# Key products and values of a recurrence kept with its two heads exchanged, on the off-diagonal 64x64 tiles of TensorE

## The reference, cut to what matters

```
def step(state, inp):
    r_t, w_t, k_t, v_t, a_t, b_t = inp
    sa = einsum("bhij,bhj->bhi", state, a_t)
    state = state * w_t + sa[..., None] * b_t + v_t[..., None] * k_t
    return state, einsum("bhij,bhj->bhi", state, r_t)
```

## Time and profile before

| | |
|---|---|
| median of 3 runs | 3216.4 us (3216.02 to 3230.35) |
| the profiled execution, its own time | 3214.21 us |
| its span, first to last instruction | 3212.4 us |
| TensorE matmul busy | 2920.5 us, 91% |
| VectorE busy | 1461.4 us, 45% |
| ScalarE busy | 438.4 us, 14% |
| mean granted TensorE clock | 0.956 |

### The profile page before, as it was taken

One profiled execution on the slowest core, in us unless ns is written; L12 is line 12 of the kernel. 1 busy time (PEld: TensorE's weight loads), 2 busy tenths in 40 slices (PEclk: granted clock), 3 DMA queues, 4 the chain that ended last, 5 costly groups with the idle time before them and its releaser, 6 DMA issues.

```text
span 3212.4 us, 50284 instructions
## 1 busy us (share of the span) xinstructions
PE 2920.5 (91%) x22141; PEld 2107.7 (66%) x22141; DVE 1461.4 (45%) x2546; ACT 438.4 (14%) x860; POOL 261.9 (8%) x372
## 2 busy tenths in 40 slices
PE   4997999999999888889979979999999998886998
PEld 4775877777775544367757758777777745443775
DVE  3542265566655756213025323656664567552001
ACT  0000132121211112000000001312111122120000
POOL 6000011001100101010000010101010010000000
PEclk7998999999999989989989989999998999998999
DMA  8782332112225432363548724322222263323342
GB/s 310 275 313 105 125 129 98 67 52 97 77 71 185 138 133 79 131 255 127 173 172 317 261 99 143 112 70 73 70 77 70 70 226 125 130 79 131 121 146 100
DMA packets 226043, 444.09 MB, mean 138 GB/s; under 512 B 7432, under 2 KB 102214, under 8 KB 225824
## 3 DMA queue, kind: packets, MB, share of 16 engines
q1 hardware_dynamic: 211136, 395.59, 34.8%
q0 software_dynamic: 12960, 38.98, 3.7%
q10 hardware_dynamic: 1728, 6.29, 0.5%
HBM read 422.88 MB, written 17.96 MB: 137 GB/s over the span
## 4 chain that ended last, share of the span: by engine, by line
PE 69%; DVE 14%; issue 10%; DMA 4%; ACT 2%; POOL 1%; SPq 0%; DVEq 0%; POOLq 0%; ACTq 0%
PE ps L966 67%; DVE scratch L1868 5%; DVE scratch L1871 2%; DVE scratch L1874 2%; DMA ring<-in_ffn_w 2%; DMA scratch<-fill_scratch 1%; DVE merged L2067 1%; DVE hT L1871 1%; ACT scratch L1566 1%; DVE scratch L2081 1%; DVE gbc L1874 1%; DMA scratch<-acs_scratch 1%; DMA ring<-in_w_in 0%; PE ps L998 0%; DVE x L1868 0%
## 5 line engine op out<-in xcount | busy, mean ns | idle before, releaser
L966 PE MATMUL ps<-hT,ring 128*128 128x256 f32 (+1 forms) x4992 | 1169.4, 389 | 32.5 <-DVE hT L1871 31.0
L966 PE MATMUL ps<-scratch 64*64 64x32 f32 (+6 forms) x14112 | 1023.9, 260 | 89.0 <-ACT scratch L1815 27.9
L966 PEld LDWEIGHTS ps<-hT,ring 128*128 128x128 f32 (+1 forms) x4992 | 941.0, 192 | 199.2 <-DVE hT L1871 33.1
L966 PEld LDWEIGHTS ps<-scratch 64*64 64x64 f32 (+2 forms) x14112 | 717.7, 145 | 433.3 <-issue 243.4
L1868 DVE TENSOR_TENSOR scratch<-scratch,ps 128x256 f32<-128x256 f32 (+3 forms) x304 | 153.5, 505 | 933.1 <-ACT scratch L1576 671.6
L966 PE MATMUL ps<-ring,hT 128*128 128x256 f32 (+1 forms) x1280 | 433.0, 485 | 6.6 <-DVE hT L2491 4.9
L966 PEld LDWEIGHTS ps<-ring,hT 128*128 128x128 f32 x1280 | 239.6, 195 | 157.3 <-issue 129.5
L1868 DVE TENSOR_TENSOR scratch<-scratch 128x512 f32<-128x512 f32 (+5 forms) x438 | 288.3, 658 | 73.2 <-DMA scratch<-acs_scratch 26.3
L966 PE MATMUL ps<-ring,scratch 128*128 128x512 f32 x512 | 239.4, 607 | 2.9 <-DVE scratch L1871 2.3
L1874 DVE SCALAR_TENSOR_TENSOR scratch<-scratch,ccol 128x1024 f32<-128x1024 f32 x126 | 164.2, 1303 | 4.5
L966 PEld LDWEIGHTS ps<-ring,scratch 128*128 128x128 f32 x512 | 95.5, 196 | 98.8 <-issue 93.3
(11 more groups left out here) (217 smaller groups left out, 1440.4 us busy)
## 6 DMA issues: line engine op xcount, KB each, us to landing
ring<-in_w_in SPq DMA_DIRECT2D x56, 2048.0 KB, 7.9
ring<-in_ffn_w SPq DMA_DIRECT2D x88, 1024.0 KB, 9.9
scratch<-in_ada_w SPq DMA_DIRECT2D x36, 2048.0 KB, 14.3
scratch<-in_ffn_w SPq DMA_DIRECT2D x44, 1024.0 KB, 4.9
scratch<-acs_scratch POOLq DMA_DIRECT2D x32, 512.0 KB, 4.9
ring<-in_w_branch_mamba SPq DMA_DIRECT2D x8, 2048.0 KB, 8.6
scratch<-fill_scratch SPq DMA_DIRECT2D x4, 2048.0 KB, 13.6
ring<-in_w_branch_rwkv SPq DMA_DIRECT2D x4, 2048.0 KB, 11.0
```

The lines of the kernel that those rows point to most:

```text
L966: return pe.matmul(o, lhsT, rhs, start=start, stop=stop)
```

## The change

A second helper, `by_other_head`, addresses the off-diagonal 64x64 tiles: with `to_other` the result of a head lands on the other head's partitions, and without it the operands of the other head's partitions give the result on a head's own. The keys' products (`kdec`) and the transposed values (`vtm`) are written to the other head's partitions, and `values_share` brings them back. So `mk`, `ktm` and `vtm` are kept with the heads exchanged. The `kdec` products are issued between the `bdec` and the `ar` product of each chunk; for d=1 all of these wait for `m2_evac` too. In the recurrent steps the value products are issued among the products on the diagonal tiles: the state's share moves from behind the u product to behind the s hand-over, the next r's share goes between the two u products, and all output shares of the values stand in j=0's first group. ScalarE's and VectorE's programs are the same.

```diff
+                def by_other_head(o, lhsT, rhs, start=True, stop=True, to_other=False):
+                    for h in range(2):
+                        hh, oh = slice(L * h, L * h + L), slice(L - L * h, 2 * L - L * h)
+                        at, of = (oh, hh) if to_other else (hh, oh)
+                        ins = mm(o[at], lhsT[of], rhs[of], start, stop)
+                    return ins
...
-                        by_head(ps[:, 0, c * L:(c + 1) * L], rkv[:, 16 + q, c * L:(c + 1) * L], stack_i[:, :])
+                        by_other_head(ps[:, 0, c * L:(c + 1) * L], rkv[:, 16 + q, c * L:(c + 1) * L], stack_i[:, :], to_other=True)
...
                             pe.wait_ge(*btm_evac(l, u))
+                            pe.wait_ge(*m2_evac(l, u))
                         for c in range(CH):
                             bank, at = 2 + c // 2, (c % 2) * 3 * L
-                            by_head(ps[:, bank, at:at + 3 * L], bdec[:, d, c, :], ar[:, d, c, :, :].rearrange("p u t -> p (u t)"))
+                            moving = ar[:, d, c, :, :].rearrange("p u t -> p (u t)")
+                            by_head(ps[:, bank, at:at + 3 * L], bdec[:, d, c, :], moving)
+                            keys = by_other_head(ps[:, 2 + bank, at:at + 3 * L], kdec[:, d, c, :], moving, to_other=True)
+                            if c == CH - 1:
+                                keys.then_inc(m2_done.sem, 1)
                             at = 6 * L + (c % 2) * L
                             ins = by_head(ps[:, bank, at:at + L], ar[:, d, c, 0, :], bdec[:, d, c, :])
                         ins.then_inc(m1_done.sem, 1)
-                        if d:
-                            pe.wait_ge(*m2_evac(l, u))
-                        for c in range(CH):
-                            bank, at = 4 + c // 2, (c % 2) * 3 * L
-                            ins = by_head(ps[:, bank, at:at + 3 * L], kdec[:, d, c, :], ar[:, d, c, :, :].rearrange("p u t -> p (u t)"))
-                        ins.then_inc(m2_done.sem, 1)
...
-                        return by_head(o, weights, vtm[:, c, :], start, stop)
+                        return by_other_head(o, weights, vtm[:, c, :], start, stop)
...
+                    def state_share(j, d):
+                        c = chunk(d, j)
+                        values_share(ps[:, 0, d * L:(d + 1) * L], ktm[:, d, c, :], c, d == 0, False)
...
                                 by_head(ps[:, 6, c * L:(c + 1) * L], ar[:, d, c, 1, :], st8[:, j, d, :], False, False)
+                                if j < CH - 1:
+                                    state_share(j, d)
                         else:
-                            for c in range(CH):
-                                values_share(ps[:, 6, c * L:(c + 1) * L], mk[:, 0, c, L:2 * L], c, c == 0, False)
+                            for d in range(2):
+                                for c in range(CH):
+                                    values_share(ps[:, 6, c * L:(c + 1) * L], mk[:, d, c, L:2 * L], c, d == 0 and c == 0, False)
+                            for d in range(2):
+                                state_share(j, d)
                         fill(p, f"r{j}")
                         pe.wait_ge(*r_evac(l, 4 * p + j + 1))
                         for d in range(2):
-                            ins = by_head(ps[:, 5, d * L:(d + 1) * L], dd[:, d, 1, chunk(d, j), :], rs[:, d, :])
-                        ins.then_inc(u_done.sem, 1)
-                        if j < CH - 1:
-                            for d in range(2):
+                            if d and j < CH - 1:
                                 c = chunk(d, j + 1)
                                 values_share(ps[:, 4, d * L:(d + 1) * L], mk[:, d, c, 0:L], c, d == 0, False)
-                            for d in range(2):
-                                c = chunk(d, j)
-                                values_share(ps[:, 0, d * L:(d + 1) * L], ktm[:, d, c, :], c, d == 0, False)
+                            ins = by_head(ps[:, 5, d * L:(d + 1) * L], dd[:, d, 1, chunk(d, j), :], rs[:, d, :])
+                            if d == 0 and j < CH - 1:
+                                c = chunk(d, j + 1)
+                                values_share(ps[:, 4, d * L:(d + 1) * L], mk[:, d, c, 0:L], c, d == 0, False)
+                        ins.then_inc(u_done.sem, 1)
...
-                        if j == 0:
-                            for c in range(CH):
-                                values_share(ps[:, 6, c * L:(c + 1) * L], mk[:, 1, c, L:2 * L], c, False, False)
```

## The result

The changed kernel takes 3253.9 us (median of 4 runs, 3249.8 to 3260.6), the kernel before 3220.6 beside it (4 runs, 3216.0 to 3230.4): a ratio of 1.0101, with a 95% interval of 1.007 to 1.0133. It is 1.0% slower, where the forecast was 3208 with a range up to 3234. The profiled execution took 3253.6 us against 3214.2, so there are 39.4 us to explain.

A forecast was written before the change was run, and what follows sets the result against it. TensorE held 69% of the chain that ended last, VectorE 14%, the two alternating in the score part. 3214.2 - 17.5 (scores and steps) + 9 (clock) = 3205.7, with 2.2 to the median 3208 us; range 3192 to 3234.

The forecast's parts named there:

- Four tiles together: Score part and recurrent steps: off-diagonal products among diagonal ones cost 0; d=1 score group about 1.9 us, not 3.2.
- the rival with only wide products: Recurrent steps: narrow 64-column products gain nothing from four tiles, only wide ones hide; 3227 us, chance 0.13.
- The rivals in which off-diagonal products cost time: Score part and steps: only wide products hide, 3227 us, chance 0.13; or no overlap at all, 3252 us, chance 0.13.
- the one at 3252: Score part and steps: off-diagonal tiles don't overlap at all; 3252 us, +1.1%, chance 0.13.
- The rule on row groups: TensorE: weight loads overlap matmuls in flight only where the row group differs, so exchanged products would not hide; 3252 us.
- Pairs without a fall: Score part -2.68 us and recurrent steps -6.06 us a layer, -17.5 us for both layers, before any clock effect.
- The new wait before the d=1 scores: Pairs 2 to 7: TensorE idles 2.2 to 2.4 us; eight clock falls in twelve gaps, +9 us (0 to +21).
- the line on pairs 2 to 5: Score part: d=1 scores -0.67 + 1.04 = +0.37 us a pair, +1.48 in all; VectorE sets the levels.
- the second 1.30: Score part, pairs 2 to 5: TensorE's 1.30 us saving for the other d, said to vanish because VectorE sets the levels.
- The other side's mechanism: Levels: clock falls there would each hold the whole chain back; given as a way to go wrong, without size or chance.
- the slower rival: Score part and steps: no overlap of off-diagonal tiles, 3252 us, +1.1%, chance 0.13.

The follow-up runs named there:

- old_order_gap: Kernel before the change, with three filling products moved from ahead of the levels to three other places, nothing packed: 3300.3 us, ratio 1.0249.
- scores_gap_closed: Changed kernel with five filling products moved to between d=0 and d=1, four from ahead of the scores, one from the end: 3285.1 us, ratio 1.0211.
- after_refilled: Changed kernel with filling moved from ahead of the scores, the end and two step places to both gaps, d=1 scores and levels: 3187.1 us, ratio 0.9924.
- levels_denser: Changed kernel with four filling products moved from ahead of the scores into four rounds of the levels, one each: 3252.2 us, ratio 1.0111.
- after_tuned: after_refilled with the filling products of r1 and u1 in the recurrent steps moved to s2: 3199.5 us, ratio 0.9938 to the kernel before.
- steps_tuned: steps_alone with two more filling products each between d=0 and d=1 and ahead of the levels, from end, r0 and u3: 3191.3 us, ratio 0.9915.
- levels_gap_closed: Changed kernel with three filling products moved from ahead of the scores to ahead of the levels: 3253.1 us, ratio 1.0105.
- steps_alone: Changed kernel with the key products back behind the scores, on off-diagonal tiles, recurrent steps as changed: 3215.2 us median of ten, ratio 0.9922 of seven runs.

## Why the prediction was wrong

- **Four tiles together: right.** 1.91 us for the d=1 group (forecast about 1.9), 0.39 for a u group (0.38), 1.54 for the first group of j=0 (1.54). The u group also takes away the ground of the rival with only wide products, which started from 29 ns a record: less 0.15 for emptying, its 16 records take 0.24 us, 15 ns each. The rivals in which off-diagonal products cost time are out, the one at 3252 too: it would have shown 3.2 us for the group. The Trainium skill's "TensorEngine Tiling (Array Packing)", section "Key Properties", has the tiles operate independently, with weight loads and matmuls of different tiles in parallel; these rows agree. The rule on row groups that the prediction cites from "TensorE: Matmul & The Clock Gate" doesn't hold for them.
- **Pairs without a fall: nearly right.** Pair 0 is 3.24 us shorter (60.69 against 63.93; forecast 3.30), pair 6 1.45 (1.63), pair 1 2.09 (1.33), and pair 7 up to its last 64x64 group 1.95 in the second layer (59.74 against 61.69; forecast 1.16). In pair 1 more of TensorE's time was in the way of the levels than I took: the end of the levels comes 1.46 us earlier after the `vtm` copy (36.38 against 37.84), forecast 0.63. In pair 2 the d=1 scores start 13.14 us after the `vtm` copy and were due after 12.66 before: +0.48 with what the steps shift, +0.46 by the start of the levels, forecast +0.37. From j=0's first product to the `vtm` copy, pair 1 took 22.01 us and takes 21.38: -0.63, forecast -0.70. A small slip: by the earlier trace rows a 64-column product is (0.84 - 0.38)/4 = 0.115 us and not 0.1175, which moves the sum by some 0.1 us a layer.
- **The new wait before the d=1 scores: right in place and size, wrong in what it does.** It is 2.48 us (forecast 2.2 to 2.4), released by VectorE. In twelve such gaps the clock fell twice, for 3.4 us, in pair 3 of each layer, and that cost 0.7 us each. The forecast was eight falls and 9 us.
- **The step that failed** is in the score part, in the line on pairs 2 to 5: "VectorE's chain after `m1` and its taps set the levels (TensorE's 0.70 wait), so the second 1.30 vanishes." As a term of the critical path that is right: TensorE's saving ahead of the levels gains nothing. But a saving that vanishes on an engine becomes idle time on it. The numbers for it were in the forecast: the wait of 0.70 and the 1.30 saved make 2.00, and 1.99 was measured. I took the clock's risk for the wait ahead of the scores alone and costed this one at nothing. It stands at the mouth of the levels, where TensorE goes on with 32-column products on diagonal tiles, from the wait to their end 17.5 us at the full clock (pair 3) and 29 at half of it (pair 2). There a fall of the clock lasts until they are over and costs 12 to 14 us, where the forecast had 1.2 us for a fall. The other side's mechanism was thus named in the prediction's last sentences ("if the falls of the clock lie in the levels"), but had no rival, price or chance of its own. Six such falls, some 80 us together, are more than the whole loss of 39.4: without them, by the sum above, the kernel would have been faster. That the measured 3254 lies beside the 3252 of the slower rival is chance.
- **What settles it:** old_order_gap brings the same long falls with the old order and a 1.98 us wait, scores_gap_closed shortens the other wait and has more of them, pairs 6 and 7 have the other wait alone and none, and after_refilled keeps the whole packing with 0.70 us ahead of the levels and has none.

**What stays open.** How long a wait at the levels may be: 1.98 to 1.99 us gave a long fall in 22 of 22 places (6, 8 and 8), but 1.44 to 2.94 us none over 20.5 us where the levels held more filling (levels_denser), 1.07 in seven of eight in one execution while other executions of that kernel were 76 us faster, 0.70 in one of eight before and one of eight in after_tuned, 0.22 in one of eight in steps_tuned, 0.38 in one of levels_gap_closed. Each of these counts is from one profiled execution a kernel. So the wait is not all that counts, and what stands before it may matter: pair 3 of the changed kernel escaped with a short fall at its scores and a wait of 0.86. The 13.7 us falls late in pair 2 are unexplained. The packed scores with the old steps were not tried, so their worth alone is open.

## What to carry to other kernels

A saving on an engine that then waits for another is not worth nothing: on TensorE the longer wait can cost the clock, and the cost is set by what comes behind it. So for each gap add the old wait and the time saved ahead of it, and ask what runs next; here a gap ahead of full-width products was cheap (0.7 us a fall), one ahead of a long run of thin products dear (12 to 14 us). When an order changes, the amount of filling work at each place has to be set anew in the same change, and taken from a place where it doesn't open the next gap: here the counts alone moved the time from +1.0% to -0.8%, and the kernel before gained 0.5% by its counts too.

## What the runs showed of the hardware

- Four 64x64 tiles of TensorE work at once, float32, weight loads included: 48 records of up to 192 columns in 1.91 us, where two tiles took 3.22. Products written behind others on busy tiles start ahead of their turn: with the keys behind the scores the same 48 records took 2.84 us.
- The length of a stretch at 0.50 depends on what TensorE does in it. It was mostly 3.4 us at the d=1 scores, where full-array filling comes next, and 27 to 34 us among the 32-column products of the levels, with two filling products in each round; there it rose again at or shortly behind the end of the levels. With three filling products in four of the rounds instead of two it was at most 20.5 us, and 6.8 us behind the longest wait (2.94).
- A wait of 2.48 us behind full-array products and ahead of packed score products made the clock fall in 2 of 12 places, one of 3.56 us in 19 of 24 (two kernels), and one of 1.99 us behind full-array filling and ahead of the levels in 22 of 22, with two filling products a round; with three, one of 1.96 had no fall (levels_denser). One of 1.41 us ahead of the packed scores, with 13 filling products before it, had none in 24 places (scores_gap_closed and after_refilled).
- A kernel can sit on the edge: steps_alone gave times of 3177 to 3259 us in ten runs on one chip, in three clusters some 38 us apart.
